# Gating layernorm of the second block: per-token sums on ScalarE behind the transposes, in place of a layernorm ahead of them

## The reference, cut to what matters

```python
v = _layernorm(v, sg_norm_g, sg_norm_b)        # over the 256 features of each token
# in each chunk of 128 tokens, for each of 4 groups of 64 features:
mixed[c, i, f] = sum_j sg_w[group(f), i, j] * v[c, j, f] + sg_b[group(f), i]
out = u * mixed

def _layernorm(x, g, b):
    mu = mean(x, axis=-1); var = mean((x - mu) ** 2, axis=-1)
    return (x - mu) * rsqrt(var + EPS) * g + b
```

## Time and profile before

| | us |
|---|---|
| median of 3 runs | 2766.63 |
| the three runs | 2766.63, 2755.2, 2766.84 |
| the profiled execution, its own time | 2758.92 |
| its span, first to last instruction | 2757.0 |
| TensorE busy in the span | 2546.5 (92%) |
| VectorE busy | 1498.7 (54%) |
| GpSimd busy | 1047.7 (38%) |
| ScalarE busy | 728.1 (26%) |

### The profile page before, as it was taken

One profiled execution on the slowest core, in us unless ns is written; L12 is line 12 of the kernel. 1 busy time (PEld: TensorE's weight loads), 2 busy tenths in 40 slices (PEclk: granted clock), 3 DMA queues, 4 the chain that ended last, 5 costly groups with the idle time before them and its releaser, 6 DMA issues.

```text
span 2757.0 us, 33015 instructions
## 1 busy us (share of the span) xinstructions
PE 2546.5 (92%) x12016; PEld 2044.8 (74%) x12016; DVE 1498.7 (54%) x2191; ACT 728.1 (26%) x1208; POOL 1047.7 (38%) x493
## 2 busy tenths in 40 slices
PE   8999999999989879999996999979899999999997
PEld 4888777777767757877674777868577777777775
DVE  4795155757501166545697644466764444444446
ACT  4411334344300155122321444432220000000112
POOL 2344333333257423447641011113553333334444
PEclk9999999999999889999998799989999999999999
DMA  8575444444365942333311231341211111111111
GB/s 345 186 260 216 157 143 138 136 134 148 118 237 196 350 165 99 99 121 119 132 39 44 69 98 58 100 152 47 69 61 46 46 46 46 46 46 46 46 46 69
DMA packets 131232, 325.24 MB, mean 118 GB/s; under 512 B 11568, under 2 KB 59248, under 8 KB 125616
## 3 DMA queue, kind: packets, MB, share of 16 engines
q1 hardware_dynamic: 91232, 215.63, 23.7%
q10 hardware_dynamic: 39888, 108.08, 10.9%
HBM read 248.57 MB, written 70.39 MB: 116 GB/s over the span
## 4 chain that ended last, share of the span: by engine, by line
PE 50%; DVE 8%; issue 3%; ACT 1%; DMA 0%; DVEq 0%; SPq 0%; ACTq 0%
PE pb L478 36%; PE g L2980 6%; PE g L3053 2%; PE pb L2980 1%; PE g L3033 1%; DVE zcs L2245 1%; PE g L2961 1%; DVE f_spare L2454 1%; PE g L2834 1%; DMA kept_in<-cs_d 0%; DVE xl L2157 0%; PE g L2959 0%; DVE hl L2524 0%; DVE x L2596 0%; DVE ml L2461 0%
## 5 line engine op out<-in xcount | busy, mean ns | idle before, releaser
L841 POOL TENSOR_TENSOR w_hi<-w_raw,one 128x1024 fp32r<-128x1024 f32 x191 | 394.8, 2067 | 1531.9 <-PE pb L478 1135.3
L844 POOL TENSOR_TENSOR w_lo<-w_raw,w_hi 128x1024 fp32r<-128x1024 f32 x191 | 511.3, 2677 | 15.0
L478 PE MATMUL pb<-xh,w_hi 128*128 128x512 f32 (+1 forms) x1224 | 482.5, 394 | 25.7 <-POOL w_lo L844 11.8
L478 PE MATMUL pb<-xh,w_lo 128*128 128x512 f32 (+1 forms) x1224 | 474.0, 387 | 0.0
L478 PE MATMUL pb<-xl,w_hi 128*128 128x512 f32 (+1 forms) x1224 | 473.9, 387 | 0.0
L478 PE MATMUL pb<-mh,w_hi 128*128 128x512 f32 x704 | 282.0, 400 | 14.9 <-DVE ml L2461 7.3
L478 PEld LDWEIGHTS pb<-xh,w_hi 128*128 128x128 f32 x1224 | 233.5, 191 | 81.4 <-POOL w_lo L844 13.6
L478 PE MATMUL pb<-mh,w_lo 128*128 128x512 f32 x704 | 279.9, 398 | 0.0
L478 PE MATMUL pb<-ml,w_hi 128*128 128x512 f32 x704 | 279.8, 397 | 0.0
L478 PEld LDWEIGHTS pb<-xl,w_hi 128*128 128x128 f32 x1224 | 232.8, 190 | 51.0
L478 PEld LDWEIGHTS pb<-xh,w_lo 128*128 128x128 f32 x1224 | 233.8, 191 | 49.6 <-issue 1.0
(11 more groups left out here) (408 smaller groups left out, 4617.9 us busy)
## 6 DMA issues: line engine op xcount, KB each, us to landing
w_raw<-in_wall SPq DMA_DIRECT2D x190, 512.0 KB, 3.6
mod_later<-in_modw SPq DMA_DIRECT2D x28, 1024.0 KB, 6.5
proj_d<-stage ACTq DMA_DIRECT2D x40, 512.0 KB, 2.7
at_bias<-in_bias SPq DMA_DIRECT2D x64, 192.0 KB, 2.6
mod_raw<-in_modt SPq DMA_DIRECT2D x8, 1024.0 KB, 11.2
w_raw<-in_wall ACTq DMA_DIRECT2D x15, 512.0 KB, 7.3
svt<-vt_d ACTq DMA_DIRECT2D x12, 512.0 KB, 4.6
vc<-proj_d SPq DMA_DIRECT2D x10, 512.0 KB, 5.6
```

The lines of the kernel that those rows point to most:

```text
L478: mm = pe.matmul(pb[bank][:, 0:n], w[:, b, wc:wc + P], x[:, k, tokens], start=(count == 0), stop=(count == total - 1))
L841: nc.gpsimd.tensor_tensor(w_hi[:, b, :], w_raw[:, b, :], one[:, 0:1].to_broadcast([P, 1024]), ALU.mult).then_inc(w_high, 1)
L844: nc.gpsimd.tensor_tensor(w_lo[:, b, :], w_raw[:, b, :], w_hi[:, b, :], ALU.subtract).then_inc(w_split, 1)
```

## The change

The layernorm is no longer made feature-major. The 16 transposes go first, on the raw `v`. With tokens on partitions a token's sum over 256 features is a sum along the free dimension, and ScalarE makes it while it copies a chunk of 128 tokens out of PSUM (`accum_out`), and the sum of squares likewise. Mean, root and reciprocal are columns of 8 numbers (`vstat`). Scale and shift by them are again one ScalarE pass over `vtok`. The gain is applied behind the product with `sg_w`, in what was the addition of `sg_b`; the bias goes into `sgb_sb`, by the sums of `sg_w` over its tokens, which four small matmuls make. Both calls of `gating_means` go. SyncE's bias loads wait for the squares (`y_act`) instead. Nothing else is changed, the loads of raw weights by ScalarE included.

```diff
+        vstat = keep("vstat", [P, 4, NCX])
-        vsq, b = at("vsq", [P, 2, T], a)
-        vroot, _ = at("vroot", [P, T], a)
+        vsq, b = at("vsq", [P, NCX, C], a)
...
-            sp.wait_ge(y_pe, 2)
-            sp.wait_ge(y_dve, 3)
+            sp.wait_ge(y_act, 2)
...
+            act.wait_ge(y_pe, 2)
+            for n in range(NCX):
+                v = act.activation(vtok[:, n, :], g[:, n // 2, C * (n % 2):C * (n % 2) + C], ACT.Copy,
+                                   accum_out=vstat[:, 0, n:n + 1])
+            v.then_inc(y_act, 1)
             pair_k_high(0, 0, pair_unit(u_k))
             act.wait_ge(y_dve, 1)
-            act.activation(vsq[:, :, :], zcs[:, 6:8, :], ACT.Square).then_inc(y_act, 1)
+            act.wait_ge(xl_ready, 6 * KT)
+            for n in range(NCX):
+                v = act.activation(vsq[:, n, :], vtok[:, n, :], ACT.Square, bias=vstat[:, 0, n:n + 1],
+                                   accum_out=vstat[:, 1, n:n + 1])
+            v.then_inc(y_act, 1)
+            act.wait_ge(y_act, 2)
+            act.activation(vstat[:, 1, :], vstat[:, 1, :], ACT.Sqrt, scale=1.0 / C,
+                           bias=epsc[:, 0:1]).then_inc(y_act, 1)
             for n in (1, 2):
                 pair_k_high(0, n, pair_unit(u_k + n))
-            act.wait_ge(y_pe, 2)
-            act.activation(vroot[:, :].rearrange("p (u n) -> p u n", u=2), g[:, 4:6, :], ACT.Sqrt,
-                           bias=epsc[:, 0:1]).then_inc(y_act, 1)
             pair_values(0, 0, pair_unit(u_v), bank_free[u_v % 2])
             keys_across(0)
             pair_values(0, 1, pair_unit(u_v + 1), bank_free[(u_v + 1) % 2])
             act.wait_ge(y_dve, 3)
-            for t in range(2):
-                n, m = COL["sg_g"] + t, COL["sg_b"] + t
-                v = act.activation(zcs[:, 6 + t, :], zcs[:, 6 + t, :], ACT.Identity,
-                                   scale=col[:, n:n + 1], bias=col[:, m:m + 1])
+            for n in range(NCX):
+                v = act.activation(vtok[:, n, :], vtok[:, n, :], ACT.Identity, scale=vstat[:, 1, n:n + 1],
+                                   bias=vstat[:, 2, n:n + 1])
             v.then_inc(y_act, 1)
             pair_values(0, 2, pair_unit(u_v + 2), bank_free[u_v % 2])
-            act.wait_ge(y_pe, 3)
-            act.activation(vtok[:, :, :].rearrange("p (a n) c -> p a (n c)", a=4), g[:, 0:4, :],
-                           ACT.Copy).then_inc(y_act, 1)
...
             taps(5, 14)
+            nc.vector.tensor_scalar(vstat[:, 3, 0:2], col[:, COL["sg_b"]:COL["sg_b"] + 2], float(C), None, ALU.mult)
+            dve.wait_ge(y_act, 1)
+            nc.vector.tensor_scalar(vstat[:, 0, :], vstat[:, 0, :], -1.0 / C, None, ALU.mult).then_inc(y_dve, 1)
+            dve.wait_ge(y_dve, 1)
             dve.wait_ge(y_pe, 1)
             for t in range(2):
-                v = nc.vector.tensor_tensor(zcs[:, 6 + t, :].rearrange("p (u n) -> p u n", u=2),
-                                            zcs[:, 6 + t, :].rearrange("p (u n) -> p u n", u=2),
-                                            g[:, 4:6, :], ALU.subtract)
-            v.then_inc(y_dve, 1)
+                nc.vector.scalar_tensor_tensor(sgb_sb[:, t, :], g[:, 4, P * t:P * t + P], vstat[:, 3, t:t + 1],
+                                               sgb_sb[:, t, :], ALU.mult, ALU.add)
             for n, (first, last) in enumerate(((14, 17), (17, 18), (18, 20))):
                 pair_k_low(0, n, pb[(u_k + n) % 2], bank_free[(u_k + n) % 2])
                 taps(first, last)
-            dve.wait_ge(y_act, 2)
-            nc.vector.reciprocal(vroot[:, :], vroot[:, :]).then_inc(y_dve, 1)
+            dve.wait_ge(y_act, 3)
+            nc.vector.reciprocal(vstat[:, 1, :], vstat[:, 1, :]).then_inc(y_dve, 1)
             dve.wait_ge(y_dve, 2)
-            nc.vector.tensor_tensor(zcs[:, 6:8, :], zcs[:, 6:8, :],
-                                    vroot[:, :].unsqueeze(1).to_broadcast([P, 2, T]), ALU.mult)\
-              .then_inc(y_dve, 1)
+            nc.vector.tensor_tensor(vstat[:, 2, :], vstat[:, 0, :], vstat[:, 1, :], ALU.mult).then_inc(y_dve, 1)
...
             evicted(pe, UNIT[T_PAIR])
-            gating_means(zcs[:, 6:8, :])
+            pe.wait_ge(sg_in, 32)
+            for q in range(4):
+                t, r = q // 2, 64 * (q % 2)
+                mm = pe.matmul(g[r:r + 64, 4, P * t:P * t + P], mean_v[:, 0:64], sgw_sb[:, q, :], start=True,
+                               stop=True)
+            mm.then_inc(y_pe, 1)
+            for n in range(NCX):
+                for t in range(2):
+                    o = (2 * n + t) * P
+                    mm = pe.transpose(g[:, o // H, o % H:o % H + P], zcs[:, 6 + t, CH * n:CH * n + CH], ident)
+            mm.then_inc(y_pe, 1)
             pe.wait_ge(xl_ready, 6 * KT)
             pe.wait_ge(xh_ready, 6 * KT)
             pe_tile(pe, T_PAIR)
-            pe.wait_ge(y_act, 1)
-            pe.wait_ge(y_dve, 1)
-            gating_means(vsq[:, :, :])
             pe_tile(pe, T_PAIR + 1)
-            pe.wait_ge(y_act, 3)
-            for n in range(NCX):
...
             pe_tile(pe, T_PAIR + 2)
             pe.wait_ge(z_cv, 2 * TAPS)
-            pe.wait_ge(y_act, 4)
+            pe.wait_ge(y_act, 1)
             conv_means(zcs[:, 0:2, :])
```

More of the change, by code:

```diff
@@ L1479, in _ @@
                 if n == 0:
-                    act.wait_ge(y_pe, 4)
+                    act.wait_ge(y_pe, 3)
                 pair_k_high(1, n, pair_unit(u_k1 + n))
@@ L2294, in _ @@
             at_stage(0)
-            dve.wait_ge(y_pe, 4)
-            dve.wait_ge(sg_in, 32)
+            dve.wait_ge(y_pe, 3)
             for t in range(2):
-                v = nc.vector.tensor_tensor(
+                n = COL["sg_g"] + t
+                v = nc.vector.scalar_tensor_tensor(
                     zcs[:, 6 + t, :].rearrange("p (n q) -> p n q", q=CH),
-                    g[:, 2 * t:2 * t + 2, :].rearrange("p a (n q) -> p (a n) q", q=CH),
-                    sgb_sb[:, t, :].unsqueeze(1).to_broadcast([P, NCX, CH]), ALU.add)
+                    g[:, 2 * t:2 * t + 2, :].rearrange("p a (n q) -> p (a n) q", q=CH), col[:, n:n + 1],
+                    sgb_sb[:, t, :].unsqueeze(1).to_broadcast([P, NCX, CH]), ALU.mult, ALU.add)
             v.then_inc(y_dve, 1)
@@ L2883, in conv_means @@
                 mm.then_inc(z_pe, 1)
[L2885 to L2890, removed]
-            evicted(pe, UNIT[T_PAIR])
-            gating_means(zcs[:, 6:8, :])
-            pe.wait_ge(xl_ready, 6 * KT)
-            pe.wait_ge(xh_ready, 6 * KT)
-            pe_tile(pe, T_PAIR)
-            pe.wait_ge(y_act, 1)
-            pe.wait_ge(y_dve, 1)
-            gating_means(vsq[:, :, :])
-            pe_tile(pe, T_PAIR + 1)
-            pe.wait_ge(y_act, 3)
+            evicted(pe, UNIT[T_PAIR])
+            pe.wait_ge(sg_in, 32)
[4 more added lines that the diff above has]
+            mm.then_inc(y_pe, 1)
             for n in range(NCX):
@@ L2906, in _ @@
             mm.then_inc(y_pe, 1)
+            pe.wait_ge(xl_ready, 6 * KT)
+            pe.wait_ge(xh_ready, 6 * KT)
+            pe_tile(pe, T_PAIR)
+            pe_tile(pe, T_PAIR + 1)
             pe_tile(pe, T_PAIR + 2)
             pe.wait_ge(z_cv, 2 * TAPS)
-            pe.wait_ge(y_act, 4)
+            pe.wait_ge(y_act, 1)
             conv_means(zcs[:, 0:2, :])
@@ L2914, in gating_products @@
                 pe.wait_ge(z_dve, 1)
-                pe.wait_ge(sg_in, 32)
+                pe.wait_ge(y_act, 4)
                 for n in range(NCX):
```

## The result

The changed kernel takes 2736.89 us in the median of 4 runs (2732.97 to 2737.56), the kernel before 2764.48 (4 runs): a ratio of 0.9907, interval [0.9881, 0.9933]. It is 26 us faster by the ratio (27.6 between the medians), where 9 were forecast and 2744 was the lower end of the range. The profiled execution took 2737.56 us, its span is 2735.8.

What follows compares the result with a forecast made beforehand. VectorE was taken as the bound from 1432 to 1499 us. Nothing from the subtraction, 8.2 from reciprocal and product, and the detour less GpSimd's conflict summed to 9 off 2766.63: 2757 us forecast, range 2744 to 2765.

Steps and rivals of the forecast that it cites:

- What bounds the kernel: VectorE bounds the stretch from 1432 to 1499 us, with one detour of 4.84 us through TensorE.
- Step 1: Subtraction on VectorE behind taps(5, 14): 1.3 us saved but swallowed, since the next taps wait for GpSimd's low part; gain 0.
- the first rival: Tiny VectorE operations behind taps(5, 14) wait for GpSimd, taps begin 2.3 us later: 6.7 gained, 2760 us; chance 0.22.
- Step 2: Reciprocal and product on VectorE behind taps(18, 20): 8.7 us become 0.5 on columns of 8 numbers; gain 8.2.
- Step 3: Detour through TensorE ahead of Q0 vanishes, but GpSimd's split falls into taps(20, 23): 8.8 to 10.0 us earlier, 11 without conflict.
- The opening: TensorE's start of the stage, transposes and four small matmuls replacing the first means: about 1.4 us earlier, buying nothing.
- ScalarE's passes: Copies with sums 3.6 us, squares 4, scalings 3.2 (0.40 each): all covered, by 5 us or so at the tightest.
- The prediction's own sign: The forecast is wrong if taps(18, 20) on VectorE end before 1454 or after 1459 us.
- the starting point: The kernel before, taken as the median of the runs shown, 2766.63 us, from which 9 was subtracted.
- The second and third rival: TensorE's low-clock stretch behind the stage: halved, 15 gained, 2751 us (chance 0.13); or lengthened by six slow steps, 2772 (0.05).

Runs made afterwards that it cites:

- both again: The kernel before and the changed kernel, each unchanged, run again with profiles on one chip: 2763.43 and 2738.0 us.
- e1_pad128: The kernel before with 128 unused bytes ahead of all large buffers, behind the weight buffers: 2750.06 us, ratio 0.9961.
- e2_arena_back: The changed kernel with vstat put into the stage's own memory, so the large buffers stand where they stood before: 2746.66 us, ratio 0.9952.
- e5_all_128: The kernel before with 128 unused bytes ahead of everything, the weight buffers included: 2760.73 us, ratio 1.0003.
- e8_pad256: The kernel before with 256 unused bytes ahead of the large buffers: 2755.64 us, ratio 0.9988.
- e9_64_64: The kernel before with 64 unused bytes ahead of the weight buffers and 64 more behind them: 2727.58 us, ratio 0.9878.
- e7_both: The changed kernel with vstat in the stage's own memory and 64 unused bytes ahead of the large buffers: 2718.86 us, ratio 0.9846 against the kernel before.

## Why the prediction was wrong

- **What bounds the kernel** was right: E to C fell by 9.2 us (before and after) and 9.3 (both again), with 9 forecast; it is 66.9 to 68.4 us in all eight profiles with the old layernorm and 57.6 to 58.1 in all five with the new one. The reciprocal put back takes 5.6 of it away.
- **Step 1**, the subtraction worth nothing: right. I had expected the taps to wait for GpSimd's low part; instead most of the wait fell on the tensor_scalar, for the high part, as in the first rival. That rival had the place right and the price wrong: it added 2.3 us because it let both tiny operations wait, while the second slipped in between the two halves of the split.
- **One row was misread**: the prediction takes the 1.90 us of the high part at 1505.97 as GpSimd's time "while VectorE waits". VectorE had begun an operation just before:

```profile
1505.69 2.29 DVE L2275 TENSOR_TENSOR zcs<-zcs,g 128x2048 f32<-128x2048 f32 x1 [6.30 <-PE g L2881]
```

It has one operand in PSUM (`g`), and the two ran side by side. No term of the sum hangs on it, but this operation of VectorE was not in GpSimd's way.

- **Step 2**: 8.2 us forecast, 8.2 measured (8.7 less 0.55).
- **Step 3**: the conflict in taps(20, 23) was forecast at 11.5 us and took 11.06 in one profile; in the other the taps took less (8.90) and VectorE waited 2.66 us for Q0, with nearly the same end (E to C 57.65 and 58.07).
- **The opening** of TensorE and **ScalarE's passes** were covered, as said. The eight scalings took 0.5 us each and not 0.40; it cost nothing.
- **The step that failed** is the sentence "nothing ahead of it on VectorE changes" with its sequel "after 1490 the rest is the same work in the same order". I took the 128 bytes of `vstat` for free and did not ask what stands behind them. The distance from one matmul to the next got 4.4 ns shorter ahead of the stage and behind it, a term that the sum had at nothing. That brought 11 us by itself (e1_pad128), and with the 14.5 of e2_arena_back it comes to 25.5, against 23.1 for the changed kernel on the same chip. The prediction's own sign for this came true: taps(18, 20) ended at 1450.28, before 1454, though 23.8 us behind taps(5, 14), as forecast. Another 2 us of the miss lie in the starting point, 2766.63, where the median of four runs is 2764.48. What is left, 3 us on that chip (23.1 - 11 - 9) and 6 in the first result (26 - 11 - 9), is open; the clock behind the stage may be in it.
- **The second and third rival**, the clock, were real, and both directions occur: in the profile of the changed kernel the stretch was longer by 3.7 us, in the repeated one the same, in e2_arena_back shorter by 5. I forecast that it would keep its length within 2 us; from C to the same step X it was 69 us before, and 63 to 73 in the others. This may be why the 9.3 us at C are 14.5 at the end of e2_arena_back, but it isn't shown: e5_all_128 and e8_pad256 have the short length with the old layernorm, and where both kernels have it (e9_64_64 and e7_both), the whole kernel gains 8.7 us. The forecast of 9 for the stage was right there, for its own reasons.

## What to carry to other kernels

Before one credits an edit with its time, one compares a stretch that the edit does not touch: the mean distance between matmuls far from the change separates work from placement. A small buffer put in front of large ones is an edit of every address behind it; kernels are to be compared with the large buffers pinned. And the place is worth tuning for itself: in this kernel 64 bytes were worth 33 us, the rewritten layernorm 9 to 14.5.

## What the runs showed of the hardware that I had not expected

- fp32r matmuls of 512 columns, each with its own weight load, follow each other at 227.2, 228.9, 232.5 or 233.3 ns at the full granted clock, by the distance of the moving from the stationary operand in their partition, modulo 256 bytes (0, 64, 128, 192), between 1200 and 1330 us. From 2200 to 2500 us the last two are alike (1261 matmuls each). Four residues were tried, in steps of 64. Why is open: whether the matmul's read and the load of the next weights meet somewhere in memory was not tested.
- The kernels with the faster matmuls get more of the low clock: ahead of 1400 us those with 227 to 229 ns have 105 to 120 us at half clock in their records, those with 232 to 233 ns 82 to 89, in all fourteen profiles. Part of the gain is given back there.
- The same work behind an idle TensorE (C to X) took 63 to 64, 69 to 70 or 73 us, and one and the same kernel took two of these lengths in two executions (72.79 and 69.17).
